# Differential attention: the turned weights and the values as pairs of half-precision parts, with three products in place of one 32-bit product

## The reference

```python
def diff_attention(q, k, v, rel_bias, lam, lam_init, subln_w):
    ...
        logits = jnp.einsum('bqhmd,bkhmd->bhmqk', q_blk, k).astype(jnp.float32) * scale + bias
        p = jax.nn.softmax(logits, axis=-1)
        attn = p[:, :, 0] - lam * p[:, :, 1]
        return jnp.einsum('bhqk,bkhd->bqhd', attn.astype(v.dtype), v)
```

## Time and profile before

| | |
|---|---|
| median of 3 runs | 3618.75 us (3616.66 to 3625.5) |
| the profiled execution, its time | 3623.91 us |
| its span in the profile | 3621.8 us |
| granted TensorE clock, mean share of 2.4 GHz | 0.968 |
| busy: TensorE matmul / VectorE / ScalarE / GpSimd | 92% / 52% / 39% / 15% |
| attention stages (steps 0 to 31) | about 2085 to 2370 us and 2868 to 3169 us |

### The profile page before, as it was taken

The page is one execution under the profiler, slowest core; times in us unless marked ns, Lnnn a source line. Parts: engine busy times, 40 slices in busy tenths (PEclk is TensorE's granted clock), DMA queues, the critical chain, the costliest instruction groups (busy, mean ns, idle before and its releaser), DMA issues. The chain is left out here.

```text
span 3621.8 us, 72693 instructions
## 1 busy us (share of the span) xinstructions
PE 3336.3 (92%) x32106; PEld 2077.5 (57%) x32106; DVE 1879.8 (52%) x2548; ACT 1401.6 (39%) x2022; POOL 551.8 (15%) x350
## 2 busy tenths in 40 slices
PE   7998999989799898999998899889889999799889
PEld 3445666654344345989994466657434566557334
DVE  4764666652345624656653466644352366634342
ACT  3553544432365522333333455523222355523211
POOL 3000000010000002333430223100240233100330
PEclk9998999989899999999999999999999999999999
DMA  5101111022235633111103211020120210020211
GB/s 169 35 24 56 41 29 41 23 75 77 82 88 128 145 101 95 65 65 65 56 32 106 64 41 35 1 64 24 44 91 15 70 41 30 1 69 19 72 53 47
DMA packets 308338, 215.35 MB, mean 59 GB/s; under 512 B 125412, under 2 KB 283951, under 8 KB 305455
## 3 DMA queue, kind: packets, MB, share of 16 engines
q1 hardware_dynamic: 307608, 210.70, 19.4%
q10 hardware_dynamic: 442, 0.37, 0.0%
HBM read 173.26 MB, written 41.98 MB: 59 GB/s over the span
## 5 line engine op out<-in xcount | busy, mean ns | idle before, releaser
L142 PE MATMUL psum<-u,w_hi 128*128 128x512 f16 x2816 | 852.1, 385 | 63.0 <-DMA mix_pool<-pool_w 24.3
L142 PE MATMUL psum<-u,w_lo 128*128 128x512 f16 x1408 | 540.5, 384 | 0.0
L142 PEld LDWEIGHTS psum<-u,w_hi 128*128 128x128 f16 x2816 | 278.4, 99 | 409.2 <-issue 45.3
L97 POOL TENSOR_TENSOR w_hi<-stage,w_scale 128x1024 f16<-128x1024 f32 x52 | 100.1, 1924 | 1246.1 <-PE psum L142 594.7
L986 PE MATMUL psum<-w_hi,merged 128*128 128x512 f16 x768 | 238.6, 391 | 29.4 <-PEq L2922 9.1
L2510 DVE CUSTOM_DVE_ANT_0 probs_att<-psum,bias_att 128x1024 f32<-128x1024 f32 x128 | 156.8, 1225 | 167.1 <-PE psum L2322 166.9
L115 DVE SCALAR_TENSOR_TENSOR w_lo<-stage,w_hi 128x1024 f16<-128x1024 f32 x124 | 149.2, 1220 | 171.5 <-ACT w_hi L109 171.3
L142 PEld LDWEIGHTS psum<-u,w_lo 128*128 128x128 f16 x1408 | 139.5, 99 | 171.5 <-issue 9.6
L2300 PE MATMUL psum<-u,w_hi 128*128 128x512 f16 x768 | 231.9, 384 | 6.3 <-PEq L1013 6.3
L986 PE MATMUL psum<-held_hi_out,merged 128*128 128x512 f16 x768 | 231.0, 379 | 0.0
L157 PE MATMUL psum<-w_hi,u 128*128 128x128 f16 x2048 | 173.2, 219 | 0.0
(11 more groups left out here) (443 smaller groups left out, 6767.9 us busy)
## 6 DMA issues: line engine op xcount, KB each, us to landing
stage<-w_in SPq DMA_DIRECT2D x72, 512.0 KB, 3.9
X<-rwkv_chunks SPq DMA_DIRECT2D x14, 1792.0 KB, 7.8
stage<-ab_w_in SPq DMA_DIRECT2D x48, 512.0 KB, 4.9
stage<-rw_w_in SPq DMA_DIRECT2D x32, 512.0 KB, 4.3
rwkv_chunks<-work_rp SPq DMA_DIRECT2D x26, 512.0 KB, 5.7
stage<-w_out SPq DMA_DIRECT2D x24, 512.0 KB, 6.0
X<-x SPq DMA_DIRECT2D x16, 512.0 KB, 11.2
stage<-ab_w_out SPq DMA_DIRECT2D x16, 512.0 KB, 6.8
```

The costliest lines, as they stand in the source:

```text
L97: pool.tensor_tensor(K.w_hi[:, slot, :], K.stage[:, slot, :], scale, ALU.mult).then_inc(K.w_half[slot], 1)
L142: last = pe.matmul(K.psum[:, bank, :], w[:, k, :], u[:, k, cols], start=(k == 0 and n == 0), stop=(k == KT - 1 and n == 2))
```

## The change

The values are split at eviction like q and k (scale 64), the turned weights are split at their eviction from T_BANK (scale 512): ScalarE writes the high part, VectorE then makes the low part from the same bank, and only that frees the bank. The product becomes 12 f16 matmuls per call in place of four 32-bit ones. The sums are unscaled when ScalarE takes them. VectorE makes the low part of v (`low` for slot 2), which it did not do before.

```diff
-        q, k = ([split(late_slots[n][:, a, :]) for n in range(2)] for a in range(2))
-        v, gate = ([late_slots[n][:, a, :] for n in range(2)] for a in (2, 3))
+        q, k, v = ([split(late_slots[n][:, a, :]) for n in range(2)] for a in range(3))
+        gate = [late_slots[n][:, 3, :] for n in range(2)]
...
-        turned = sb("turned", [P, 2, 4, P])
+        turned_hi, turned_lo = (sb(n, [P, 2, 4, P], F16) for n in ("turned_hi", "turned_lo"))
...
                     for n in range(4):
-                        last = pe.matmul(K.psum[:, O_BANK, (i % 4) * P:(i % 4 + 1) * P],
-                                         v_tiles[h % 2][:, half * 4 + n, :], turned[:, half, n, :],
-                                         start=(half == 0 and n == 0), stop=(half == 1 and n == 3))
+                        for m, (a, b) in enumerate(((v_hi, turned_hi), (v_hi, turned_lo), (v_lo, turned_hi))):
+                            last = pe.matmul(K.psum[:, O_BANK, (i % 4) * P:(i % 4 + 1) * P],
+                                             a[:, half * 4 + n, :], b[:, half, n, :],
+                                             start=(half == 0 and n == 0 and m == 0),
+                                             stop=(half == 1 and n == 3 and m == 2))
...
                 def take_turned(s, half):
                     act.wait_ge(turn_done, 2 * s + half + 1)
-                    act.copy(turned[:, half, :, :].rearrange("p n q -> p (n q)"),
-                             K.psum[:, T_BANK, :]).then_inc(turned_ready, 1)
+                    act.mul(turned_hi[:, half, :, :].rearrange("p n q -> p (n q)"), K.psum[:, T_BANK, :],
+                            ATTN_SCALE).then_inc(turned_high, 1)
...
-                    if slot < 2:
-                        hi, lo = (q, k)[slot][g % 2]
-                        dve.wait_ge(high_ready, (g * 2 + slot) * 2 + half + 1)
+                    if slot < 3:
+                        hi, lo = (q, k, v)[slot][g % 2]
+                        dve.wait_ge(high_ready, (g * 3 + slot) * 2 + half + 1)
...
+                def low_turned(s, half):
+                    dve.wait_ge(turned_high, 2 * s + half + 1)
+                    dve.scalar_tensor_tensor(turned_lo[:, half, :, :].rearrange("p n q -> p (n q)"),
+                                             K.psum[:, T_BANK, :], ATTN_SCALE,
+                                             turned_hi[:, half, :, :].rearrange("p n q -> p (n q)"),
+                                             ALU.mult, ALU.subtract).then_inc(turned_ready, 1)
...
                 with_bias(0)
+                for half in range(2):
+                    low(0, 2, half)
                 with_bias(1)
...
                 for s in range(N):
                     if s + 2 < N:
                         with_bias(s + 2)
+                    low_turned(s, 0)
                     if s + 1 < N:
                         combine(s + 1)
+                    low_turned(s, 1)
```

More of the change, by code:

```diff
@@ L2188 @@
 A_HEADS = 4
-Q_SCALE, K_SCALE = 8.0, 64.0
+Q_SCALE, K_SCALE, V_SCALE, ATTN_SCALE = 8.0, 64.0, 64.0, 512.0
+VALUE_UNSCALE = 1.0 / (V_SCALE * ATTN_SCALE)
 LOGIT_UNSCALE = 0.125 / (Q_SCALE * K_SCALE)
@@ L2217, in diff_attention @@
         split = lambda x: (x.bitcast(F16)[:, 0:S], x.bitcast(F16)[:, S:2 * S])
-        q, k = ([split(late_slots[n][:, a, :]) for n in range(2)] for a in range(2))
-        v, gate = ([late_slots[n][:, a, :] for n in range(2)] for a in (2, 3))
-        v_tiles = [x.rearrange("p (t c) -> p t c", t=TT) for x in v]
+        q, k, v = ([split(late_slots[n][:, a, :]) for n in range(2)] for a in range(3))
+        gate = [late_slots[n][:, 3, :] for n in range(2)]
+        v_tiles = [[x.rearrange("p (t c) -> p t c", t=TT) for x in parts] for parts in v]
         probs = sb("probs", [P, 2, 2, S])
         attn = sb("attn", [P, 2, S])
-        turned = sb("turned", [P, 2, 4, P])
+        turned_hi, turned_lo = (sb(n, [P, 2, 4, P], F16) for n in ("turned_hi", "turned_lo"))
         bias = sb("bias", [P, 2, SKEW])
@@ L2235, in diff_attention @@
             sem("logits_done"), sem("logits_taken"), sem("max_ready"), sem("probs_ready"), sem("attn_ready"))
-        turn_done, turned_ready, o_done, o_taken = (
-            sem("turn_done"), sem("turned_ready"), sem("o_done"), sem("o_taken"))
+        turn_done, turned_high, turned_ready, o_done, o_taken = (
+            sem("turn_done"), sem("turned_high"), sem("turned_ready"), sem("o_done"), sem("o_taken"))
         norm_done, norm_taken, rs_ready, m_ready, hi_ready, part_done = (
@@ L2241, in diff_attention @@
         cols = lambda half: slice(half * HALF, (half + 1) * HALF)
-        scales = (UNSCALE * Q_SCALE, UNSCALE * K_SCALE)
+        scales = (UNSCALE * Q_SCALE, UNSCALE * K_SCALE, UNSCALE * V_SCALE)
         def unit_of(s):
@@ L2348, in values @@
                         pe.wait_ge(o_taken, s // 4)
+                    v_hi, v_lo = v_tiles[h % 2]
                     for n in range(4):
-                        last = pe.matmul(K.psum[:, O_BANK, (i % 4) * P:(i % 4 + 1) * P],
-                                         v_tiles[h % 2][:, half * 4 + n, :], turned[:, half, n, :],
-                                         start=(half == 0 and n == 0), stop=(half == 1 and n == 3))
+                        for m, (a, b) in enumerate(((v_hi, turned_hi), (v_hi, turned_lo), (v_lo, turned_hi))):
[3 more added lines that the diff above has]
+                                             stop=(half == 1 and n == 3 and m == 2))
                     if i % 4 == 3 and half == 1:
@@ L2403, in evict @@
                         act.wait_ge(half_done, g * 4 + slot + 1)
-                    if slot < 2:
-                        act.mul((q, k)[slot][g % 2][0][:, cols(half)], bank, scales[slot]).then_inc(high_ready, 1)
-                    elif slot == 2:
-                        act.mul(v[g % 2][:, cols(half)], bank, UNSCALE).then_inc(taken[half], 1)
+                    if slot < 3:
+                        act.mul((q, k, v)[slot][g % 2][0][:, cols(half)], bank, scales[slot]).then_inc(high_ready, 1)
                     else:
@@ L2431, in take_values @@
                         act.wait_ge(part_done, part - 1)
-                    act.copy(O[:, cols(part % 2)], K.psum[:, O_BANK, :])
-                    act.activation(sq[:, cols(part % 2)], K.psum[:, O_BANK, :], ACT.Square).then_inc(o_taken, 1)
+                    act.mul(O[:, cols(part % 2)], K.psum[:, O_BANK, :], VALUE_UNSCALE)
+                    act.activation(sq[:, cols(part % 2)], K.psum[:, O_BANK, :], ACT.Square,
+                                   scale=VALUE_UNSCALE).then_inc(o_taken, 1)
                 def rstd(part):
@@ L2491, in low @@
                     bank = K.psum[:, PROJ + half, :]
-                    if slot < 2:
-                        hi, lo = (q, k)[slot][g % 2]
-                        dve.wait_ge(high_ready, (g * 2 + slot) * 2 + half + 1)
+                    if slot < 3:
+                        hi, lo = (q, k, v)[slot][g % 2]
+                        dve.wait_ge(high_ready, (g * 3 + slot) * 2 + half + 1)
                         dve.scalar_tensor_tensor(lo[:, cols(half)], bank, scales[slot], hi[:, cols(half)], ALU.mult,
                                                  ALU.subtract).then_inc(taken[half], 1)
-                    elif slot == 3:
+                    else:
                         x = gate[g % 2][:, cols(half)]
```

## The result

The changed kernel takes 3641.03 us (median of 5 runs, 3638.3 to 3646.19) against 3622.79 for the kernel before, run beside it on the same chip: a ratio of 1.0053, 95% interval 1.0041 to 1.0065, or **18.2 us slower**. The forecast was +7.5 us (3626); the time lies inside the range, but not in the case "within 0.3%" that had the largest chance.

The account below looks back on a forecast made before the run. TensorE was taken to bound steps 0 to 23, the chain from logits to product the last head. Per attention -4.8 + 8.5 = +3.7, twice +7.5 us, gave 3626 us against the median 3618.75; range 3612 to 3646.

Parts of the forecast that it names:

- within 0.3%: Whole kernel: the case that the time stays within 0.3% (11 us) of the kernel before; chance 0.52.
- Point 1: Product in steps 0 to 23: a `values` call takes 0.67 us for 0.89, together -10.3 us an attention.
- Point 2: Steps 0 to 23: low_turned(s,0) just fits before turn(s,1); 0.5 us an attention, between 0 and 4.
- Point 3: Steps 7, 15, 23: gated ends late, high_part delays the copy; stall 1.67 us, +5.0 an attention (0 to 8).
- Regime one: Steps 0 to 23, where projection pieces fill TensorE: -10.3 + 0.5 + 5.0 = -4.8 us an attention.
- Point 4: Last head, steps 24 to 31: VectorE becomes the bound; last take_values at 63.15 us, +8.5 an attention (+5.5 to +12).
- Point 5: low_turned beside GpSimd: with one input in PSUM it takes its usual 0.69 us, so nothing is charged.
- Point 6: Prologue and ends: low(0,2) of v costs 0, uncovered 2 x 0.69 us; the stage after attention starts as before.
- low_turned sets the pace in every step: Rival, steps 0 to 23: margin 0.05 us; a chain 0.25 us later gives +19 us, 3638; chance 0.37.
- Waits for GpSimd: Rival: low_turned waits for GpSimd's L101, turn(s,1) late by 2.0 or 1.1 us, +43 us, 3662; chance 0.03.
- a last head over 68 us: Sign of a wrong forecast: last head under 57 or over 68 us to the last take_values.
- with_bias to with_bias of 6.5 to 8 us: Sign of a right forecast: in the last head, successive with_bias starts lie 6.5 to 8 us apart.

Follow-up runs that it names:

- e2: Changed kernel with 12 f16 matmuls per call, but the low part of the turned weights neither made nor used; 3604.28 us.
- e5: Changed kernel with one line moved: ScalarE does high_part after take_turned(s,0), not first in its step; 3628.72 us.
- e1: Changed kernel with the product back as one 32-bit matmul; VectorE still makes the low parts, which nothing reads; 3649.19 us.
- e3: Changed kernel plus blocks of eight unread f16 filler matmuls on TensorE before turns, norms and last values of the last head; 3634.72 us.
- e6: Changed kernel with the last head left as before the change (32-bit product, no low part); 3617.32 us.
- e9: Changed kernel with a 32-bit last head, high_part after take_turned(s,0), and an own bank for turn(s,1) in the last head; 3591.78 us.
- e10: Changed kernel with high_part after take_turned(s,0) and an own bank for turn(s,1) in the last head, no fillers; 3609.43 us.
- e8: Changed kernel with high_part after take_turned(s,0), an own bank for turn(s,1) in the last head, and filler matmuls from step 25 on; 3622.97 us.

## Why the prediction was right, and where it was wrong

**Point 1, the product:** right. 0.67 a call and steps of 8.91 (8.90 forecast); e2 gives 9.9 for 10.3. The source was TensorE's own v projection in the same form. The Trainium skill, "TensorE: Matmul & The Clock Gate", Part 1, gives 55.6 ns from start to start at 128 columns at the full clock; 0.67 / 12 = 0.056 us agrees.

**Point 2, the low part between two turns:** right for steps 1 to 23. low_turned(s,0) is ready 0.12 before the turn in steps like 10 and the turn stays at 5.11; e5, with low parts but no stall, takes 212.8 for steps 1 to 23; e2, with no low parts, takes 212.6 once its three longer steps are counted as the others, so the low parts cost some 0.3 there. The step that failed is small: step 0 has no values(-1,1), so its second turn was due at 4.4 and waited for low_turned until 5.04. That costs 0.66 an attention (8.89 against 8.23 in e2); 0.5 had been put down for all steps.

**Point 3, gated late:** right. Stall 1.6 in steps 7, 15, 23 (1.67 forecast); e5 removes 4.75 (5.0 forecast). Regime one in all: -4.6 + 0.44 = -4.2, forecast -4.8. That steps 1 to 23 agree to the tenth is luck: the product saved 9.6 for the 10.1 laid out for them, and stalls and low parts cost 5.0 for 5.5.

**Point 4, the last head:** right in mechanism, wrong in size, and this is the term that made +18 out of +7.5. It said +8.5 an attention, bounds +5.5 to +12 "if two more half clock episodes" came; it measured +15.0 and +14.6, outside the bounds, with another 1 us behind the last take_values, where the last norm also ran at half clock. Each interval had been laid out at the clock of the kernel before, and the clock was treated as a mishap with a count, not as something that the change moves. It moves it in two ways at once: the product leaves TensorE 0.22 us less work a call, and low_turned lengthens the waits between the calls. e1 (product long again, clock 0.92 and 0.95, 64.8 us) and e3 (fillers, 1.00 and 0.97, 64.5 us) both land, in the mean of their two last heads, within 2 us of the forecast's 63.15; the changed kernel is at 69.1. The product alone (e2) does little to the clock, 0.87 and 0.90, and lengthens nothing: it takes both.

**Point 5, the shared port:** right. All 128 low_turned took 679 to 693 ns, in the steps with L101 beside them too:

```profile
L2536 DVE SCALAR_TENSOR_TENSOR turned_lo_att<-psum,turned_hi_att x128: 679/691/693, 2082.3 to 3179.4; 128x512 f16<-128x512 f32 x128
```

The rule of "SBUF — State Buffer" in the Trainium skill ("Who interferes with whom"), that a VectorE instruction with at most one SBUF input, outside the two-port modes, does not contend with GpSimd, agrees with that. The small two-input operation (now L2525) even takes less time, 34.7 us in all for 49.4, because it starts 0.6 later in GpSimd's shadow. That, and the 0.08 by which each record overlaps the next operation, is why VectorE's busy time grew by 74.2 and not by the 99 forecast.

**Point 6 and the stages behind:** cost 0 in the prologue holds. The retention is 2 us shorter than before in the profile (203.5 and 203.6 for 205.9 and 205.6), but the change needn't be the cause: in all thirteen profiles the stage takes either 203.3 to 204.0 or 205.4 to 205.9 us, and e3, e5, e6, e9 and e10 each show both lengths in one execution. What decides between them stays open.

**The rivals.** "low_turned sets the pace in every step" held the weight of the slower cases, and did not happen: its place kept its margin. "Waits for GpSimd" did not happen, and the change does what it says. The slower case came through the last head alone, which that rival carried only as a side remark ("with a last head at +12"). That rival's working has a slip besides: by its own margin of 0.05, a chain 0.25 us later would cost 24 x 0.20 = 4.8 an attention, not 6. Of the signs set beforehand, a last head over 68 us was the one for "wrong", and it came; with_bias to with_bias of 6.5 to 8 us there didn't hold either (11.5 and 9.3 at (28) and (31)).

That the time lies inside the range is luck in part. The forecast's own bounds ended at twice +9, or 3637; the upper end of 3646 came from rivals that did not happen. And of the 15 us between 3626 and 3641, 4 are the kernel before itself, at 3622.79 for the 3618.75 that the forecast started from.

## What to carry to other kernels

In a stretch where TensorE waits for others, its clock is part of the sum: look at the granted clock of that stretch before, and ask whether the change gives TensorE less to do or longer waits there. If it does, price the stretch with its calls at either level of the clock. Work added between a copy and the release of a bank costs next to nothing where other matmuls fill the gap (0.3 us in steps 1 to 23) and nearly its full length where none do (e1: 10.5 us for 16 low parts of 0.69), so use such a form by stage, or give that stage a second bank.

## What was not expected of the hardware

A shorter product made the last head longer: with the low parts in place, going from 32 bit (e1, 64.8 us) to half precision (after, 69.1) costs 4.3 us an attention, while the clock falls from 0.92 and 0.95 to 0.78 and 0.74. Fillers that add 1.73 us of TensorE work a time shorten it by 4.6 us where they lie in a wait (e3), and lengthen it by 6.3 us where many of them don't (e8 against e10), at a clock that rises or stays (0.94 and 0.85 to 0.95 and 0.92).
